# First loads of a hybrid encoder step: tokens in pieces of 1, 2, 3 and 2 column chunks, and one token turn moved behind the first weight products

## The reference

```python
def trunk(x, ...):
    for i in range(DEPTH):                       # 2 layers
        h = rmsnorm(x, norm_mix[i])
        ...                                      # layer 0: dsa_mixer, first step proj = h @ w_in
        ...                                      # layer 1: ssd_mixer (Mamba-2)
        x = x + out.astype(x.dtype)
        x = x + sqrelu_mlp(rmsnorm(x, norm_ffn[i]), mlp_w_up[i], mlp_w_down[i]).astype(x.dtype)
    return (rmsnorm(x, norm_final), ...)
```

## Time and profile before

| | us |
|---|---|
| median of 3 runs (1812.64 to 1812.91) | 1812.82 |
| the profiled execution | 1813.26 |
| its span in the trace | 1811.4 |
| PE busy in the span | 1784.9 |
| DVE busy | 1312.3 |
| ACT busy | 825.7 |
| first matmul of a weight product | 10.45 |

### The profile page before, as it was taken

How to read it: one execution, slowest core, us unless ns; L and a number is a source line. 1 busy time by engine, 2 the same in 40 slices (tenths; PEclk the granted TensorE clock), 3 DMA queues, 4 the chain that set the end, 5 groups by cost and what they waited for, 6 DMA issues and landing times.

```text
span 1811.4 us, 35106 instructions
## 1 busy us (share of the span) xinstructions
PE 1784.9 (99%) x13025; PEld 1690.9 (93%) x13025; DVE 1312.3 (72%) x2450; ACT 825.7 (46%) x1477; POOL 347.9 (19%) x381
## 2 busy tenths in 40 slices
PE   8999999999999999999999999999999999999998
PEld 7887668999999999999999999998999999999998
DVE  4498976468575777978788888888535766758785
ACT  4323875344343433536544655456333434334353
POOL 0002663200000000123333333432020000000011
PEclk9999999999999999999999999999999999999999
DMA  6382144333343343223444344444323433323232
GB/s 162 74 128 64 55 138 135 99 82 88 92 95 88 79 111 79 68 78 107 140 138 144 102 125 124 141 149 148 113 85 97 97 94 77 108 80 94 82 78 74
DMA packets 326708, 186.27 MB, mean 103 GB/s; under 512 B 39536, under 2 KB 319184, under 8 KB 325552
## 3 DMA queue, kind: packets, MB, share of 16 engines
q1 hardware_dynamic: 307904, 173.49, 33.9%
q0 software_dynamic: 15840, 7.87, 3.5%
q10 hardware_dynamic: 2832, 3.15, 0.5%
HBM read 164.30 MB, written 19.99 MB: 102 GB/s over the span
## 4 chain that ended last, share of the span: by engine, by line
PE 82%; DVE 2%; ACT 1%; issue 1%; DVEq 0%; ACTq 0%
PE psum L203 26%; PE psum L1449 26%; PE psum L1514 20%; PE psum L618 1%; PE psum L622 1%; PE psum L582 1%; PE psum L569 1%; PE psum L594 1%; PE psum L2748 1%; PE psum L551 0%; PE psum L2732 0%; PE psum L605 0%; PE psum L2721 0%; PE psum L563 0%; PE psum L1476 0%
## 5 line engine op out<-in xcount | busy, mean ns | idle before, releaser
L203 PE MATMUL psum<-b2H,WH 128*128 128x320 f32 x896 | 213.8, 320 | 1.2 <-DVE b2L L1247 0.7
L1514 PE MATMUL psum<-HH,HT 128*128 128x320 f32 x680 | 210.4, 309 | 3.2 <-DVE xT L1727 1.8
L1514 PE MATMUL psum<-HL,HT 128*128 128x320 f32 x680 | 210.7, 310 | 0.0
L203 PE MATMUL psum<-b2H,WL 128*128 128x320 f32 x896 | 204.1, 309 | 0.0
L203 PE MATMUL psum<-b2L,WH 128*128 128x320 f32 x896 | 203.7, 308 | 0.0
L1449 PE MATMUL psum<-b2H,HT 128*128 128x320 f32 x816 | 186.3, 309 | 0.0
L1449 PE MATMUL psum<-b2L,HT 128*128 128x320 f32 x816 | 186.1, 309 | 0.0
L191 ACT ACTIVATE WH<-W 128x1024 fp32r<-128x1024 f32 x89 | 94.0, 1056 | 193.6 <-PE psum L203 181.7
L1514 PE MATMUL psum<-HH,LT 128*128 128x320 f32 x560 | 173.5, 310 | 0.0
L203 PEld LDWEIGHTS psum<-b2H,WH 128*128 128x128 f32 x896 | 146.3, 188 | 11.2 <-issue 8.4
L1449 PE MATMUL psum<-b2H,LT 128*128 128x320 f32 x672 | 153.0, 309 | 0.0
(11 more groups left out here) (437 smaller groups left out, 4200.2 us busy)
## 6 DMA issues: line engine op xcount, KB each, us to landing
W<-ssm_w_in SPq DMA_DIRECT2D x96, 256.0 KB, 3.1
RW<-mlp_w_up SPq DMA_DIRECT2D x64, 256.0 KB, 3.0
RWx<-mlp_w_up SPq DMA_DIRECT2D x64, 256.0 KB, 3.2
RW<-mlp_w_down SPq DMA_DIRECT2D x64, 256.0 KB, 3.1
RWx<-mlp_w_down SPq DMA_DIRECT2D x64, 256.0 KB, 3.3
bc<-scratch_acs SPq DMA_DIRECT2D x8, 1280.0 KB, 7.4
W<-attn_w_in SPq DMA_DIRECT2D x32, 256.0 KB, 3.9
prev<-state_ssm SPq DMA_DIRECT2D x16, 512.0 KB, 5.4
```

The costliest lines, as they stand in the source:

```text
L203: last = pe.matmul(psum[0:m, b.out + h, 0:TH], w[:, b.slot, k, 0:m], r[:, k, h * TH:(h + 1) * TH], start=(n == 0 and i == 0), stop=(n == K ...
L1514: last = pe.matmul(down_bank(g, i), w[:, k], x[:, DNB[i], k], start=(opens and k == 0 and c == 0), stop=(k == 3 and c == 2), skip_group_ch ...
```

## The change

The four pieces in which x is loaded were 2, 2, 2 and 2 chunks of 128 columns. They become 1, 2, 3 and 2. The number of DMAs, their queue and their places in the queue stay; the contiguous run of a token row that one piece reads goes from 1024 bytes four times to 512, 1024, 1536 and 1024 bytes. The waits follow: the turn of chunk 1 now waits for the second piece, that of chunk 3 for the third, that of chunk 6 for the fourth. On PE the turn of chunk 3 moves from before to behind the products of slab 0 with chunk 0.

```diff
+    X_FROM = (0, 1, 3, 6, 8)
     x_in = [sem("x_columns_landed%d" % i) for i in range(4)]
...
             def turn_x(d):
-                if d % 2 == 0:
-                    pe.wait_ge(x_in[d // 2], 32)
+                if d in X_FROM:
+                    pe.wait_ge(x_in[X_FROM.index(d)], 32)
                 if d >= 2:
                     pe.wait_ge(x_ready, d - 1)
...
-            for d in range(4):
+            for d in range(3):
                 turn_x(d)
             first_products(0, 0)
+            turn_x(3)
             first_products(0, 1)
             turn_x(4)
...
             def load_x(i):
-                c = slice(256 * i, 256 * i + 256)
+                c = slice(P * X_FROM[i], P * X_FROM[i + 1])
```

## The result

The changed kernel takes 1815.74 us in the median of 19 runs (1814.56 to 1816.89), the kernel before, timed beside it, 1812.75 us (19 runs, 1812.07 to 1814.94). The ratio is 1.0014 with a 95% interval of 1.0008 to 1.0020: slower by 3.0 us by the medians, 1.5 to 3.6 by the interval. The forecast was 1813.3 with a range up to 1814.8.

The account below looks back on a forecast made before the run. The prediction took PE to bound the kernel and DVE its opening. Its terms summed as 0 + 0 + 0 + 0.5 + 0 = +0.5 us, so 1812.82 + 0.5 = 1813.3 us, with a range of 1811.9 to 1814.8.

Parts of the forecast that it names:

- The bound of the opening: First 30 us: DVE, busy 11.63 of 11.74 us from 8.16 to 19.90, bounds the opening; PE bounds the kernel.
- Term 1: Smaller first piece of x: first turn still waits for the norm weights until 5.51; 0, gain at most about 0.7 us.
- term 3: First slab behind three chunks: lands up to 0.95 us earlier, split gains 0.3 at most; 0 to the opening's end.
- Term 2: Turn of chunk 1 waits for the second piece, interpolated to land at 6.84; 0, between -0.4 and +0.4 us.
- Term 4: Turn of chunk 3 behind the first products: DVE stands still before copying chunk 3, +0.5 us.
- Term 5: Turn of chunk 3 waits for the third piece, landing at 11.4, wanted at 11.99: cover 0.6 us, no cost.
- The pace rival: PE's opening: idle before the first products delays the rise to full pace; +1.0 to +2.0 us, centre +1.5; chance 0.12.
- The first rival: Opening loads: norm weights and second piece land early, DVE's row begins 0.3 to 0.7 earlier; net -0.2 us; chance 0.2.
- The second: Third piece lands 0.3 to 1.0 us after 11.99, delaying the copy of chunk 3; +0.8 to +1.5 us; chance 0.17.

Follow-up runs that it names:

- e4: The changed kernel, with ACT issuing the third piece of x only behind the high part of chunk 0: 1815.33 us, ratio 1.0013.
- e7: The kernel before with only the turn of chunk 3 moved, plus 7 extra transposes filling PE's wait before the first products: 1813.48 us, ratio 1.0002.
- e1: The changed kernel's pieces 1, 2, 3, 2 with PE's old order, turn of chunk 3 ahead of the first products: 1815.75 us, ratio 1.0013.
- e2: The kernel before with its pieces 2, 2, 2, 2, only the turn of chunk 3 moved behind the first products: 1814.48 us, ratio 1.0005.
- e3: The kernel before, with the third piece issued straight after the second, without waiting for the norm weights: 1815.61 us, ratio 1.0010.
- e8: The changed kernel, with SP issuing slab 0 at 1.8 us, ahead of the one-hot table and the relative bias: 1815.97 us, ratio 1.0017.
- e10: The changed kernel with pieces of 1, 2, 2 and 3 chunks: 1815.15 us, ratio 1.0012.
- e5: The changed kernel with extra transposes in PE's waits, 9 behind the turn of chunk 0 and 18 behind that of chunk 2: 1815.74 us, ratio 1.0013.
- e6: The kernel before with 3 extra transposes behind the turn of chunk 3: 1812.97 us, ratio 1.0002.
- e9: The changed kernel with pieces of 2, 1, 3 and 2 chunks: 1814.27 us, ratio 1.0005.
- e11: The kernel before, with nine extra fp32 matmuls on PE before the norm weights are there: 1813.72 us, ratio 1.0005.
- e12: The kernel before, with the prompt part of its first piece loaded by two DMAs of one chunk (512-byte runs): 1814.83 us, ratio 1.0009.

## Why the prediction was wrong

*The bound of the opening.* Right: everything passed through DVE, and each kernel's root follows its WL start at 15.96 to 17.6 us.

*Term 1, norm weights (the step that failed).* I took 0 and put a gain of up to 0.7 beside it. They came 0.99 earlier. What I missed is that ACT waits for them too, and that its third piece of x is queued behind this wait: an earlier release brought a transfer forward into the slab's. I had listed the issue as lying at "5.50 to 6.44" as if it were fixed. This step, the place of the third piece's issue taken as given, is what turned term 3 from 0 to 2.63; its sign is reversed as well: the earlier landing made the kernel slower.

*Term 2, the second piece.* I interpolated 6.84 from the landings of before; it landed at 7.85. The interpolation took for granted that the DMA system stays saturated, and it did not (205 GB/s from 4 to 5 us). Cost: 9.28 - 8.16 = 1.12 at DVE's second copy (1.07 in e4), outside my bound of 0.4. (The 6.79 beside it should read 6.77; that changes nothing.)

*Term 3, the slab.* I had it up to 0.95 earlier and worth nothing. It came 2.63 later. The direction was wrong for the reason under term 1; this term alone is two thirds of the 3.98. The 0 that I gave it rested on ACT being the later of the two; in the changed kernel ACT had issued everything by 8.14 and waited 4.12 us for the slab.

*Term 4, the moved turn.* Right as a mechanism, DVE idle before the copy of chunk 3, released by PE, and right in size at full pace: +0.48 in e7, +0.5 in the forecast.

*Term 5.* Right by luck: the third piece landed at 4.92 + 7.6 = 12.5, later than the 11.4 of the forecast, but the turn wanted it only at 14.8. In e1, where the turn stands ahead of the products, PE waited for it until 12.59.

*The rivals.* The pace rival happened: not as an alternative to the others but on top, since the moved turn (e2) and the late slab (e3) each open a wait of PE. My +1.0 to +2.0 for it included the moved turn's 0.5; measured the same way it is 1.35, of which 0.86 (17.32 - 16.46) is pace, and 1.55 in e2: the size was right. Its condition was in my text, and giving it 0.12 was too little for a mechanism whose idle stretch the change itself makes. The first rival (the loads win) had the right observation, early norm weights, and the wrong sign. The second (the third piece late) had it too, a landing at 12.5, but this cost nothing, since the slab was later still. The cases were priced as exclusive, and the range let none of them add up. The wide range, up to +2.0, ended 0.9 short of the measured median.

*How the queues share the engines.* Beside my terms stood a rule of the Trainium skill, "DMA: Bandwidth & Descriptors", section "Queues, rings and completion order": a DMA engine takes turns between the queues, a whole packet at a time. What the traces show is where the slab's bytes move. In the kernel before, ACT's queue has moved all 1.31 MB of its first two pieces by 7.2 us and has nothing to move until 8.0, since the third piece was issued late; the slab moves in this gap. The queue rows from 7 to 8 us, SP's first:

```profile
q1 hardware_dynamic: 665, 0.33, 114.6%
q10 hardware_dynamic: 8, 0.01, 1.8%
```

In e3 the third piece follows without a gap, and in the same microsecond the slab, issued at the same time as before, gets next to nothing (ACT's queue first):

```profile
q10 hardware_dynamic: 352, 0.35, 99.9%
q1 hardware_dynamic: 83, 0.02, 8.7%
```

In the changed kernel both queues move from 9 to 10 us, and the tokens take 0.33 of 0.39 MB while the slab's last part waits (ACT's queue first):

```profile
q10 hardware_dynamic: 220, 0.33, 88.7%
q1 hardware_dynamic: 134, 0.06, 19.9%
```

This does not look like even turns, but it does not refute the rule either: the Trainium skill puts several descriptors into a packet, a packet of these rows carries one run of 1536 or 512 bytes at most, and the rows don't show when SP's queue had packets ready. How the system chooses between the queues stays open, and e8 forbids the simplest answer. On the pace, the Trainium skill, "TensorE: Matmul & The Clock Gate", section "What's actually happening", ties it to recent activity; e2 against e7, the same order with and without work in the wait, agrees with it (17.52 against 16.45).

**Where one microsecond of the loss went.** The opening lost 3.98 in the trace and the last product ends 3.94 later (1799.64 and 1803.58 its starts), but the span grew by 2.9. The 27 transposes of the output at the very end, kernel before, then the changed kernel:

```profile
1801.84 4.81 PE L1915 MATMUL psum<-cst,y_fin 128*128 128x128 f32 x27
```

```profile
1805.78 3.14 PE L1916 MATMUL psum<-cst,y_fin 128*128 128x128 f32 x27
```

After, they follow each other by 0.12 us as at full pace, before, by 0.18, and take 1.67 us longer. In e10 they took 4.81 again, and its profiled time of 1816.94 is the highest of its ten; in the eleven other kernels they took 3.14 or 3.15. No edit touches this place, so I take it as chance of the execution; what decides it was not tried. It is one part of the spread of 1.1 to 3.0 us that the runs of one kernel show. It does not explain all: in every kernel with a late root but e5 the median moved less than the root of its one trace (e3 +2.3 against +3.52, e10 +2.3 against +3.39), and why stays open.

## What to carry to other kernels

When a load is made to land earlier, list what its waiters have queued behind the wait, the DMAs above all: they will be issued earlier too and go into whatever transfer is then under way; a late wait can be what keeps two transfers apart. Don't interpolate a landing between two landings of a saturated stretch if the change empties that stretch. And when work is moved out of a wait on TensorE, price what follows at the low pace as well as the work itself: here the idle time that the change made slowed the next products, and effects that share a cause add up rather than exclude each other.

## What the runs showed of the hardware that I had not expected

- The landing of 8 KB of norm weights depends on what the other queue reads at the time: at 5.2 to 5.8 us beside a first DMA of 512 KB in runs of 1024 bytes (before, e2, e3, e6, e7, e9, e11), at 4.2 to 4.7 beside one of 256 KB in runs of 512, also where the first piece has the same bytes in all (e12: 4.34).
- Two 256 KB halves of one slab, issued half a microsecond apart, landed at 8.46 and 12.0 in the changed kernel (4.8 and 7.8 us after issue), at 8.6 and 9.3 before.
- The granted clock is printed as 1.00 in every window of these openings, while two products take 0.73 or 0.46 us and follow the pair before by 0.53 or 0.29, near half and full pace, which I read as the levels of 1.2 and 2.4 GHz. The distance of like instructions says it, the column doesn't.
- Three of the ten executions of e5, with 27 extra transposes on PE, spent 2.8 to 3.0 us around their span; the other seven spent 1.8 to 2.0, the changed kernel 1.84 in its profiled execution, e6 and e7 1.8 in all. What sets it was not tried.
